# Gate and up projection: joined halves of the activations, weights in rows of eight blocks, SwiGLU in the down projection

## The reference

```python
def swiglu(h, w_gu, w_down):
    g, u = jnp.split(h @ w_gu, 2, axis=-1)
    return (jax.nn.silu(g) * u) @ w_down
...
        hf = rmsnorm(x, norm_ffn_g[l])
        x = x + swiglu(hf, w_gu[l], w_down[l])
    return rmsnorm(x, final_norm_g)
```

## Time and profile before

| | us |
|---|---|
| median of 3 runs | 2796.68 (2795.51 to 2796.78) |
| the profiled execution | 2797.07 |
| its span, first to last instruction | 2795.2 |
| direct units and sums, up to the gate and up stage | until 1428.4 |
| gate and up stage | 1428.4 to 2296.0 |
| down projection and final norm | from 2296.0 |

### The profile page before, as it was taken

How to read it: one execution, slowest core, us unless ns; L and a number is a source line. 1 busy time by engine, 2 the same in 40 slices (tenths; PEclk the granted TensorE clock), 3 DMA queues, 4 the chain that set the end, 5 groups by cost and what they waited for, 6 DMA issues and landing times.

```text
span 2795.2 us, 40599 instructions
## 1 busy us (share of the span) xinstructions
PE 2736.9 (98%) x16062; PEld 2413.4 (86%) x16062; DVE 1755.3 (63%) x1857; ACT 1037.8 (37%) x1299; POOL 893.6 (32%) x778
## 2 busy tenths in 40 slices
PE   9999999999999999998989999999999999999997
PEld 7888888888788888897779999999999998888886
DVE  6677643345643353663688888888888885555556
ACT  6545532224532231242543333333333332222224
POOL 0000000000000003410488898898889860000000
PEclk9999999999999999999999999999999999999999
DMA  6222132222222243242323333333333344333332
GB/s 241 69 90 73 63 109 91 98 98 90 69 87 96 96 156 130 91 143 69 136 91 114 118 111 120 120 108 121 114 106 121 122 173 159 128 105 128 130 110 83
DMA packets 87894, 312.64 MB, mean 112 GB/s; under 512 B 9680, under 2 KB 13776, under 8 KB 87120
## 3 DMA queue, kind: packets, MB, share of 16 engines
q1 hardware_dynamic: 84160, 298.88, 31.1%
q10 hardware_dynamic: 3600, 11.86, 1.0%
HBM read 290.78 MB, written 19.92 MB: 111 GB/s over the span
## 4 chain that ended last, share of the span: by engine, by line
PE 74%; DVE 12%; POOL 9%; ACT 3%; issue 2%; DMA 1%; SPq 0%; DVEq 0%; POOLq 0%; ACTq 0%
PE acc L1781 14%; PE acc L1783 14%; PE acc L1782 14%; PE acc L1808 5%; PE acc L1810 5%; PE acc L1809 5%; PE ps L2158 3%; PE ps L2156 3%; PE ps L2157 3%; DVE w_lo L1560 2%; DVE cg L1650 1%; POOL over_lo L567 1%; POOL over_hi L569 1%; POOL over_lo L569 1%; POOL over_hi L570 1%
## 5 line engine op out<-in xcount | busy, mean ns | idle before, releaser
L1781 PE MATMUL acc<-act_hi,w_hi 128*128 128x512 f32 (+1 forms) x1568 | 604.4, 385 | 2.6 <-DVE w_lo L1078 1.2
L1078 DVE TENSOR_TENSOR w_lo<-raw,w_hi 128x1024 fp32r<-128x1024 f32 x328 | 428.5, 1312 | 282.4 <-ACT w_hi L603 281.7
L603 ACT ACTIVATE w_hi<-raw 128x1024 fp32r<-128x1024 f32 x328 | 344.7, 1056 | 681.9 <-PE acc L1783 343.0
L1783 PE MATMUL acc<-act_hi,w_lo 128*128 128x512 f32 (+1 forms) x1568 | 597.8, 381 | 0.0
L1782 PE MATMUL acc<-act_lo,w_hi 128*128 128x512 f32 (+1 forms) x1568 | 597.2, 381 | 0.0
L1781 PEld LDWEIGHTS acc<-act_hi,w_hi 128*128 128x128 f32 x1568 | 295.3, 188 | 60.6 <-DVE w_lo L1078 2.1
L1783 PEld LDWEIGHTS acc<-act_hi,w_lo 128*128 128x128 f32 x1568 | 295.1, 188 | 57.1
L1782 PEld LDWEIGHTS acc<-act_lo,w_hi 128*128 128x128 f32 x1568 | 295.5, 188 | 55.8 <-issue 1.0
L522 POOL MEMSET mem_stat<- 128x256 f32 x1 | 0.3, 311 | 1048.1 <-DMA mem<-mem_t 1048.1
L2156 PE MATMUL ps<-t_hi,w_hi 128*128 128x256 f32 x1120 | 317.6, 284 | 0.0
L2157 PE MATMUL ps<-t_lo,w_hi 128*128 128x256 f32 x1120 | 317.5, 283 | 0.0
(11 more groups left out here) (307 smaller groups left out, 5579.7 us busy)
## 6 DMA issues: line engine op xcount, KB each, us to landing
raw<-w_stream SPq DMA_DIRECT2D x496, 512.0 KB, 3.3
hid_t<-cg ACTq DMA_DIRECT2D x22, 512.0 KB, 2.6
over_lo<-hid_t SPq DMA_DIRECT2D x22, 512.0 KB, 4.0
x<-x_t SPq DMA_DIRECT2D x16, 512.0 KB, 8.7
x_tokens<-x_n SPq DMA_DIRECT2D x4, 1024.0 KB, 15.5
x_spill<-x SPq DMA_DIRECT2D x8, 512.0 KB, 2.9
x<-x_spill SPq DMA_DIRECT2D x8, 512.0 KB, 5.2
out_t<-x SPq DMA_DIRECT2D x7, 512.0 KB, 3.0
```

The source lines that it names most:

```text
L603: nc.scalar.activation(w_hi[:, s, :], raw[:, s, :], ACT.Copy).then_inc(hi_done, 1)
L1078: nc.vector.tensor_tensor(w_lo[:, s, :], raw[:, s, :], f(w_hi[:, s, :]), ALU.subtract)\
L1781: nc.tensor.matmul(dst, wh, ah, start=start and k == 0, stop=False)
L1783: last = nc.tensor.matmul(dst, wl, ah, start=False, stop=stop and k == UK - 1)
```

## The change

- The halves of the activations lie in one tensor, low before high (act_both, and t_both for the sums). A product of w_hi now streams both halves as 512 columns into a full bank, hi*lo in its left half and hi*hi in its right; w_lo * hi adds 256 columns to the right half. The reader adds the two halves of each bank.
- A unit's weights lie as eight blocks of 256 columns in a row (mix_raw): four loaded, four sums made in place by three GpSimd instructions. Blocks 1 to 7 are rounded by one ScalarE and subtracted by one VectorE instruction of 1792 columns. The raw places are two slots of the ring each, or a free part of over_lo; the halves are in wm_hi and wm_lo or in seven eighths of two ring slots.
- The activation sums are made by VectorE (mixed_sums).
- SwiGLU is done in the stage only for the first two pairs (INLINE). For the others, and for the direct tiles, gate and up are stored separately (gate_t, up_t), fetched as one group runs into over_lo and over_hi for the next, and multiplied there: VectorE scales both by rstd, ScalarE takes the sigmoid, GpSimd multiplies. The order of the down groups is changed (ORDER), so that the first one uses the two finished pairs.

The diff, cut:

```diff
-W11, W12, W22 = range(3)
-S3, S1, S2, S4 = range(4)
-
-
-PRODUCTS = (("w", W11, "b", B11), ("w", W12, "b", B21), ("s", S2, "t", T2), ("s", S1, "t", T1), ("s", S3, "t", T3),
-            ("s", S4, "b", B22), ("w", W22, "t", T4))
+W11, W12, W22, S3, S1, S2, S4 = range(7)
+
+
+PRODUCTS = ((W11, "b", B11), (W12, "b", B21), (S2, "t", T2), (S1, "t", T1), (S3, "t", T3), (S4, "b", B22), (W22, "t", T4))
...
+INLINE = 2
+ORDER = [*range(1, MIXES + 1), 0]
...
+            over = sb("over", [P, 2, KT, S], F32, a)
+        act_both = sb("act_both", [P, 2, KT, S], F32R)
+        act_lo, act_hi = (act_both[:, n, :, :] for n in range(2))
+        over_lo, over_hi = (over[:, n, :, :] for n in range(2))
...
+            t_both = sb("t_both", [P, 2, KT, S], F32R, a)
+        t_lo, t_hi = (t_both[:, n, :, :] for n in range(2))
...
+            wm_hi = sb("wm_hi", [P, 7, 2 * P], F32R, a)
+            wm_lo = sb("wm_lo", [P, 7, 2 * P], F32R, a)
...
+        def mix_raw(n):
+
+
+            if n % 3 == 2:
+                return over_lo[:, 0:UK, SH:S]
+            return raw[:, 2 * (n % 3):2 * (n % 3) + 2, :].rearrange("p r (b c) -> p (r b) c", b=4)
+
+        def mix_half(hi, n):
+
+            if n % 3 == 0:
+                return (wm_hi if hi else wm_lo)[:]
+            ring = (w_hi if hi else w_lo)[:].rearrange("p r (b c) -> p (r b) c", b=4)
+            return ring[:, 7 * (n % 3 - 1):7 * (n % 3), :]
...
+                    sp.wait_ge(lo_done, U_MIX + (-2, 0)[n] if n < 2 else U_MIX + n - 2)
+                sp.dma_start(mix_raw(n)[:, 0:4, :], w[U_MIX + n, :, :].rearrange("p (b c) -> p b c", b=4))\
+                    .then_inc(mix_in[n % 3], 16)
...
+            def hidden_in(g):
+
+                for b in range(0, GROUP, 2):
+                    p = ORDER[2 * g + b // 2]
+                    sp.wait_ge(gate_stored, 16 * (p + 1))
+                    sp.dma_start(over_lo[:, hid_part(g % 2, b), :], gate_t[p, :, :, :]).then_inc(hid_in[g % 2], 16)
+                    if g:
+                        sp.wait_ge(up_stored, 16 * (p - INLINE + 1 if p else 1))
+                        sp.dma_start(over_hi[:, hid_part(g % 2, b), :], up_t[p, :, :, :]).then_inc(hid_in[g % 2], 16)
...
+            def late_weights(n):
+                sp.wait_ge(lo_done, U_DOWN - 2 if n < 2 else U_DOWN - 1 if n < 4 else U_DOWN + n - RING + 1)
+                sp.dma_start(raw[:, n % RING, :], w[U_DOWN + n, :, :]).then_inc(raw_in[n % RING], 16)
...
+                part = mix_raw(n)
+                pool.wait_ge(mix_in[n % 3], 16 * (n // 3 + 1))
+                link(nc.gpsimd.tensor_tensor(part[:, 4, :], part[:, 0, :], part[:, 1, :], ALU.subtract))
+                link(nc.gpsimd.tensor_tensor(part[:, 5:7, :], part[:, 0:5:4, :],
+                                             part[:, 3:4, :].broadcast_to([P, 2, 2 * P]), ALU.add))
+                nc.gpsimd.tensor_tensor(part[:, 7, :], part[:, 2, :], part[:, 6, :], ALU.subtract).then_inc(sums_made, 1)
...
+            for g in range(1, GROUPS):
+                for b in range(0, GROUP, 2):
+                    tiles_ = hid_part(g % 2, b)
+                    hidden = over_lo[:, tiles_, :]
+                    pool.wait_ge(sig_made, INLINE + 2 * (g - 1) + b // 2 + 1)
+                    link(nc.gpsimd.tensor_tensor(hidden, hidden, sig_tmp(b), ALU.mult))
+                    pool.wait_ge(up_scaled, 2 * (g - 1) + b // 2 + 1)
+                    nc.gpsimd.tensor_tensor(hidden, hidden, over_hi[:, tiles_, :], ALU.mult).then_inc(hid_mixed, 1)
...
+                    i = converted.n - U_MIX
+                    act.wait_ge(sums_made, i + 1)
+                    act.wait_ge(unit_done, converted.n - 2)
+                    nc.scalar.activation(mix_half(True, i), mix_raw(i)[:, 1:8, :], ACT.Copy).then_inc(hi_done, 1)
                     converted.add()
...
-                    convert(RING - 2)
-                    convert(RING - 2)
-                    hidden_high(0, 32)
...
+                    act.wait_ge(hid_in[0], 32)
+                    for b in range(0, GROUP, 2):
+                        nc.scalar.activation(act_hi[:, hid_part(0, b), :], over_lo[:, hid_part(0, b), :], ACT.Copy)\
+                            .then_inc(hid_hi, 1)
+                    convert(1)
+                    convert(1)
...
+            def group(slot):
+                units(3)
+                sigmoids(slot)
+                units(3)
+                hidden_high(slot)
+                units(2)
...
+            def mixed_sums(c):
+
+                b11, b12, b21, b22 = (x[:, UK * k + 4 * c:UK * k + 4 * c + 4, SH * t:SH * (t + 1)]
+                                      for k in range(2) for t in range(2))
+                dve.wait_ge(x_gained, UK * (c + 1))
+                link(nc.vector.tensor_tensor(b22, b12, b22, ALU.subtract))
+                link(nc.vector.tensor_tensor(b12, b12, b11, ALU.subtract))
+                link(nc.vector.tensor_tensor(b11, b11, b22, ALU.subtract))
+                nc.vector.tensor_tensor(b21, b21, b11, ALU.subtract).then_inc(t_made, 1)
...
+                def half(i, h):
+                    return bank(n, i)[:, SH * h:SH * (h + 1)]
+
+                def added(to, base, product, told=link):
+                    link(nc.vector.tensor_tensor(to, product(1), base, ALU.add))
+                    told(nc.vector.tensor_tensor(to, product(0), to, ALU.add))
+
+                both_tiles = [P, 2, SH]
+                dve.wait_ge(products_done, len(TOLD) * g + 1)
+                link(nc.vector.tensor_copy(out[:, 1, :], half(0, 1)))
+                link(nc.vector.tensor_tensor(out[:, 1, :], half(0, 0), out[:, 1, :], ALU.add))
+                dve.wait_ge(products_done, len(TOLD) * g + 2)
+                added(out[:, 0:4:3, :], out[:, 1:2, :].broadcast_to(both_tiles), lambda h: two_banks(0, h), freed)
+                dve.wait_ge(products_done, len(TOLD) * g + 3)
+                added(out[:, 1:3, :], out[:, 3:4, :].broadcast_to(both_tiles), lambda h: two_banks(1, h))
+                added(out[:, 3, :], out[:, 2, :], lambda h: half(3, h), freed)
+                dve.wait_ge(products_done, len(TOLD) * g + 4)
+                added(out[:, 1, :], out[:, 1, :], lambda h: half(5, h), freed)
+                dve.wait_ge(unit_done, U_MIX + 4 * (g + 1))
+                added(out[:, 2, :], out[:, 2, :], lambda h: half(6, h), freed)
...
+            units()
+            mixed_sums(0)
+            units()
+            mixed_sums(1)
+            units()
+            mixed_low(0)
+            rstd_of(4, rstd, S)
+            mixed_low(1)
...
+                if inline:
+                    dve.wait_ge(up_stored, 16)
+                    nc.vector.tensor_tensor(cg[:], cg[:], both, ALU.mult).then_inc(gate_scaled, 1)
...
+                if last:
+                    hidden_low(0)
+                else:
+                    mix_low()
...
+                read_products(2 * p - 1, cu)
+                if inline:
+                    nc.vector.tensor_tensor(cg[:], cg[:], cu[:], ALU.mult).then_inc(hid_made, 1)
+                if last:
+                    units(3)
+                else:
+                    mix_low(4)
...
                 for n in range(KT // 2):
-                    if n == KT // 4:
+                    down(2 * n, first=first)
+                    if n == 2:
+                        dve.wait_ge(hid_in[slot], arrived[slot].at(64))
+                        for b in range(0, GROUP, 2):
+                            tiles_ = over_lo[:, hid_part(slot, b), :]
+                            nc.vector.tensor_tensor(tiles_, tiles_, both, ALU.mult).then_inc(gate_scaled, 1)
+                    if n == 3:
+                        for b in range(0, GROUP, 2):
+                            tiles_ = over_hi[:, hid_part(slot, b), :]
+                            nc.vector.tensor_tensor(tiles_, tiles_, both, ALU.mult).then_inc(up_scaled, 1)
+                        arrived[slot].add(64)
+                    if n == 6:
                         hidden_low(slot)
...
                     for j in range(2):
-                        k = ks.start + 2 * c + j
-                        ah, al = (act_hi[:, k, toks], act_lo[:, k, toks]) if kind == "b" else                             (t_hi[:, t_block(k, toks), :], t_lo[:, k, toks])
-                        cols = slice(P * (2 * block_no + j), P * (2 * block_no + j + 1))
+                        src = (act_both if kind == "b" else t_both)[:, :, ks.start + 2 * c + j, toks]
+                        cols = slice(P * j, P * (j + 1))
                         first, end = c == 0 and j == 0, c == 3 and j == 1
-                        nc.tensor.matmul(dst, blocks_hi[:, cols], ah, start=first, stop=False)
-                        nc.tensor.matmul(dst, blocks_hi[:, cols], al, start=False, stop=False)
-                        last = nc.tensor.matmul(dst, blocks_lo[:, cols], ah, start=False, stop=end)
+                        nc.tensor.matmul(dst, hi[:, w_block, cols], src, start=first, stop=False)
```

(4 more changed lines are left out.)

380 lines of the change are left out of this document (137 added, 243 removed).

## The result

The changed kernel takes 2824.28 us (median of 4 runs, 2822.55 to 2825.35), the kernel before on the same chip 2796.15 (2795.51 to 2796.78, 4 runs): a ratio of 1.010, with a 95% interval of 1.0083 to 1.0117. It is 28 us slower, inside the range on record, but a little over twice the forecast's 13.5. The profiled execution took 2823.73 us, with a span of 2821.8.

The account below looks back on a forecast made before the run. TensorE's pace was taken to bound the kernel: -30.7 (stage ends earlier) + 6.8 + 2.4 (way out) + 1 (first down group) + 34 (down groups) = +13.5, giving 2810 us, 0.5% slower; range 2780 to 2848.

Parts of the forecast that it names:

- The way in: Before direct unit 7, ahead of the gate and up stage: 5.9 us of TensorE idle and 2.4 us at half clock.
- The gate and up stage: Products 815.4 us, plus 21 us of stops at group reads and 3 us for the two in-line pairs.
- 14 x (0.2267 + 0.120) = 4.85 us: Gate and up unit: 14 products of 512 columns and 14 of 256 take 4.85 us, for 5.04 before.
- 2 x 1.2 plus what a late sigmoid adds, 3 us: Gate and up stage: cost of the first two pairs, which still multiply in line, 3 us.
- The third term, 0.5 us per group: Gate and up stage: TensorE waits for w_lo behind each group's read, 21 us in all, ends 4 and 55.
- Rival (c): Raw-slot loop replaces the read (34 us more) or GpSimd gets between up tiles (21 more): 2831 to 2865; chance 0.2.
- the 0.6 that I had given as its limit: Raw-slot loop in the stage: it decides once transfer plus sums take over 0.6 us more than reckoned.
- The way out: Before the first down product: 6.8 us of wait with restart, then 2.4 us of half clock.
- The down groups: Two stops by late additions, 2.0 and 1.4 us: 3.4 us for each of ten groups, 34 us; ends 17 and 55.
- The 1 us for the first group's transfers: First down group: four hidden transfers instead of two stand ahead of weights, 1 us, 0 to 3.
- Both mechanisms: Down groups: w_hi queued behind both sigmoids delays the addition; GpSimd's multiplications and VectorE exclude each other reading SBUF.
- eight reads of 256 columns: VectorE's read at a gate group's end, listed as one copy, eight instructions of 256 columns and four of 512.

Follow-up runs that it names:

- its run: Changed kernel with ScalarE making the next w_hi ahead of the sigmoid in the two pairs whose SwiGLU is done in the stage: 2821.57 us.
- the sigmoids' run: Changed kernel with ScalarE making w_hi of the seventh unit before the two sigmoids in each down group: 2812.13 us.
- by GpSimd's: Changed kernel with GpSimd's multiplications in the down groups cut to 2 columns of each tile, all waits kept: 2807.73 us.
- the three other edits of order: On the changed kernel, beside addition first: products high, high, low, low; w_hi before the in-line sigmoid; last direct units' w_lo earlier. All four: 2779.54 us.

## Why the prediction was right or wrong

Against its own sum (2797.07 + 13.5 = 2810.6, measured 2823.73) the result is 13.1 us over. By its steps:

- **The way in: right in its mechanism, 1.7 us too dear.** Idle 4.31 for 5.9 us, because GpSimd's sums fell beside the reciprocal (1401.42 to 1405.16) and stretched nothing in VectorE's queue, whose t_lo ended at 1410.2; half clock 1.7 for 2.4 us, some eight products at 0.43. The stage started at 1424.18 for 1425.9.
- **The gate and up stage: 855.8 for 839.4, 16.4 us over.** Here the forecast failed, in two terms. The first is **"14 x (0.2267 + 0.120) = 4.85 us"**: a pair takes 0.3507 in the mean, and (0.3507 - 0.3467) x 2352 = 9.4 us. The two paces of the earlier trace rows each hold for a row of equal products; that they add up when they alternate was taken for granted, and I weighed only whether one product costs more. The second is **"2 x 1.2 plus what a late sigmoid adds, 3 us"**, with the usual 0.5 at each of the four groups some 5 us: these four groups lose 13.6. Six stops lose 0.83, 1.34, 2.99, 1.33, 1.01 and 2.95, 10.5 us, and behind the last the granted clock was 0.50 for 3.4 us, 1.5 us more, at a place for which the sum has no half clock. I had priced the multiplication alone; but a chain of them stands ahead of w_lo in the middle of the gate group as well, w_hi is late behind the sigmoid (its run took 3.7 us off the stops), and beside GpSimd the w_lo takes 2.54 for 2.02. The third term, 0.5 us per group, held: the 38 other groups lose 17.4 us, 0.46 each, released by w_lo as forecast. Rival (c), the loop of raw slots, did not decide, though transfers took 4.1 us for my 3.3, past the 0.6 that I had given as its limit: the loop has more slack than I read from the order. Together +9.4 + 8.6 - 1.6.
- **The way out: right.** 6.86 us from the last product to the first down product and 2.4 at half clock (12 products at 0.43), for 6.8 and 2.4. The list behind the tiles was the one read from the order.
- **The down groups: right.** Stops of 1.9 and 1.23 us at the fifth and sixth unit, for 2.0 and 1.4, and 0.3 in the slow products behind them: 34.6 us in ten groups for 34. (In the tenth a half clock came in place of the second stop.) The 1 us for the first group's transfers wasn't there: besides its half clock that group loses 0.3 us, where it lost 1.6 in the kernel before. Together 1.6 us less than reckoned. Both mechanisms were confirmed apart, by the sigmoids' run and by GpSimd's.
- A slip without effect: the prediction lists eight reads of 256 columns in a group's read; the order has seven, and its 6.5 us are reckoned with seven (measured 2278.94 to 2285.46).
- -1.7 + 16.4 + 0 - 1.6 = +13.1.

By the Trainium skill (SBUF — State Buffer, "SBUF: two separate sides"), a VectorE instruction with two inputs in SBUF and a GpSimd instruction that reads SBUF shut each other out, each for a whole instruction. That held here: w_lo beside GpSimd's multiplication took 3.42 us, and the second stop went when the multiplication was cut to two columns. The 2.5 ns that the Trainium skill gives for the fixed part of a product (TensorE: Matmul & The Clock Gate, "Step-by-step: what each phase is for") did not hold for these products: where TensorE ran at its quick pace, a pair took 0.3470 us, with the 13.3 ns of the earlier trace rows in each product.

What decided the sign was read rightly: the stage's gain, given back in the down projection. What the forecast didn't see is how cheaply that could be avoided. I took VectorE's order for given; with the addition ahead of w_lo the change is worth 6.5 us, and with the three other edits of order 17.

## What to carry to other kernels

In a hand-written list, what frees a resource that the bounding engine wants next stands ahead of what is needed several steps later; work that is moved in beside the products may fit by its busy time and still cost its full length in what is queued behind it. A pace read from equal instructions is a bound for a mixed sequence, not its value: give the mixture a term of its own, with both ends. Where one edit removes a wait, look at once for the next thing in that line: the way out gave nothing, and what the way in freed was lost again in the stage.
